# The norm behind attention and the last output tile worked in two halves of the tokens, with residual updates written through a PSUM bank

## What is computed

```python
x = x + g1 * rms_norm(y_lat, mix_post_g[i])        # y_lat = o @ w_o, behind attention
f_lat = conv_ffn(modulate(rms_norm(x, ffn_pre_g[i]), sh2, sc2), *ffn)
x = x + g2 * rms_norm(f_lat, ffn_post_g[i])        # the output

def conv_ffn(h, w_up, w_dw, b_dw, w_down):
    gate, val = jnp.split(h @ w_up, 2, axis=-1)
    gate = depthwise_conv(gate, w_dw) + b_dw        # width 3, along the tokens
    return (jax.nn.gelu(gate) * val) @ w_down
```

## Time and profile before

| What | Value |
|---|---|
| three runs | 1698.0, 1706.21, 1707.32 us; median 1706.21 us |
| profiled execution | 1699.19 us, of which the span of its instructions is 1697.4 us |
| PE busy in the span | 1606.5 us (95%) |
| DVE, ACT and POOL busy | 737.4, 734.3 and 822.1 us (43, 43 and 48%) |
| chain that ended last | PE 79%, DVE 7%, issue 5%, DMA 3%, POOL 3%, ACT 2% |

### The profile page before, as it was taken

The page is one execution under the profiler, slowest core; times in us unless marked ns, Lnnn a source line. Parts: engine busy times, 40 slices in busy tenths (PEclk is TensorE's granted clock), DMA queues, the critical chain, the costliest instruction groups (busy, mean ns, idle before and its releaser), DMA issues.

```text
span 1697.4 us, 25340 instructions
## 1 busy us (share of the span) xinstructions
PE 1606.5 (95%) x9293; PEld 1283.3 (76%) x9293; DVE 737.4 (43%) x1384; ACT 734.3 (43%) x1093; POOL 822.1 (48%) x444
## 2 busy tenths in 40 slices
PE   6789999999999999999999999999996999999996
PEld 2676656769998888888888687777774888888885
DVE  3574796664457444344442714454333433333002
ACT  3431343555765555454322425454453544443221
POOL 1453334558788744444445543242524344444553
PEclk8899999999999999999999999999997999999998
DMA  9677777455565523232774231111112233233321
GB/s 385 205 211 215 208 216 215 137 186 179 180 188 151 152 93 99 87 99 83 284 267 160 83 102 45 48 39 56 45 36 77 65 97 98 88 98 93 100 80 49
DMA packets 71651, 224.82 MB, mean 132 GB/s; under 512 B 8080, under 2 KB 15760, under 8 KB 71312
## 3 DMA queue, kind: packets, MB, share of 16 engines
q1 hardware_dynamic: 68832, 215.72, 40.9%
q10 hardware_dynamic: 2736, 7.95, 1.3%
HBM read 218.13 MB, written 5.51 MB: 132 GB/s over the span
## 4 chain that ended last, share of the span: by engine, by line
PE 79%; DVE 7%; issue 5%; DMA 3%; POOL 3%; ACT 2%; SPq 1%; DVEq 0%; ACTq 0%; POOLq 0%
PE bank L1657 20%; PE bank L1655 20%; PE bank L1656 20%; PE bank L1625 2%; POOL bias L753 2%; PE bank L1975 2%; DVE bank L1316 1%; PE bank L1977 1%; DVE x_lat L1223 1%; PE bank L1976 1%; PE bank L2048 1%; PE bank L2058 1%; PE bank L1599 1%; DMA squares_lat<-in_mod_w 1%; PE bank L1818 1%
## 5 line engine op out<-in xcount | busy, mean ns | idle before, releaser
L657 POOL TENSOR_TENSOR w_lo<-w_raw,w_hi 128x1024 fp32r<-128x1024 f32 (+1 forms) x288 | 686.4, 2389 | 718.1 <-ACT w_hi L815 718.0
L815 ACT ACTIVATE w_hi<-w_raw 128x1024 fp32r<-128x1024 f32 (+1 forms) x288 | 298.8, 1038 | 239.7 <-PE bank L1657 189.7
L1657 PE MATMUL bank<-h_hi_lat,w_lo 128*128 128x512 f32 x856 | 336.9, 394 | 0.0
L1655 PE MATMUL bank<-h_hi_lat,w_hi 128*128 128x512 f32 x856 | 335.8, 392 | 0.6 <-DVE u_lat L1340 0.6
L1656 PE MATMUL bank<-h_lo_lat,w_hi 128*128 128x512 f32 x856 | 335.3, 392 | 0.0
L1655 PEld LDWEIGHTS bank<-h_hi_lat,w_hi 128*128 128x128 f32 x856 | 160.7, 188 | 49.3 <-issue 11.3
L1656 PEld LDWEIGHTS bank<-h_lo_lat,w_hi 128*128 128x128 f32 x856 | 160.7, 188 | 36.4
L1657 PEld LDWEIGHTS bank<-h_hi_lat,w_lo 128*128 128x128 f32 x856 | 160.9, 188 | 33.0
L1655 PE MATMUL bank<-h_hi_ctx,w_hi 128*128 128x256 f32 x544 | 157.2, 289 | 11.1 <-DVE h_lo_ctx L1247 7.3
L1657 PE MATMUL bank<-h_hi_ctx,w_lo 128*128 128x256 f32 x544 | 153.6, 282 | 0.0
L1656 PE MATMUL bank<-h_lo_ctx,w_hi 128*128 128x256 f32 x544 | 153.6, 282 | 0.0
(11 more groups left out here) (224 smaller groups left out, 2708.1 us busy)
## 6 DMA issues: line engine op xcount, KB each, us to landing
w_raw<-in_ffn_w_up SPq DMA_DIRECT2D x132, 512.0 KB, 3.5
w_raw<-in_cv_w_pw SPq DMA_DIRECT2D x48, 512.0 KB, 5.6
w_raw<-in_ffn_w_down SPq DMA_DIRECT2D x48, 448.0 KB, 3.4
ada_raw<-in_mod_w SPq DMA_DIRECT2D x40, 512.0 KB, 6.9
mod_rows<-in_mod_rows SPq DMA_DIRECT2D x32, 512.0 KB, 5.8
w_raw<-in_ffn_w_down SPq DMA_DIRECT2D x24, 512.0 KB, 3.6
shifted_lat<-u_lat SPq DMA_DIRECT2D x32, 270.0 KB, 6.6
w_raw<-in_na_w_qk SPq DMA_DIRECT2D x16, 512.0 KB, 4.0
```

Of the source, the lines that this page charges most:

```text
L657: pool.tensor_tensor(wlo[s][:, 0:kt * P], raw[s][:, 0:kt * P], whi[s][:, 0:kt * P].bitcast(F32), ALU.subtract).then_inc(w_lo, 1)
L815: act.activation(whi[s][:, 0:kt * P], raw[s][:, 0:kt * P], ACT.Copy).then_inc(w_hi, 1)
L1655: pe.matmul(b, whi[s][:, w], hi[:, a], start=(first and k == 0), stop=False)
L1657: ins = pe.matmul(b, wlo[s][:, w], hi[:, a], start=False, stop=(last and k == kts - 1))
```

## The change

The chain behind attention is worked in two halves of 256 tokens, and the halves are laid past one another.

- **PE.** The second round of `o` makes the first half of all four blocks, then the second half. The first half's sum of y squares and its spread are put inside the second half's matmuls. The first round of `up1` starts three blocks on the first half, with the other half's spread among them, then the fourth; the second half starts with two blocks, the first gate and value pair, which is signalled before the other pair is begun.
- **DVE, ACT, POOL.** Each step of the chain handles 256 tokens, in an order written out by hand. In the first half the scaled y is written to a PSUM bank and added to x from there. In the second half the even tiles go that way on DVE, and POOL adds the odd ones. ACT loads the table for gelu at the end of the chain, ahead of the first gate.
- **The last tile.** The eighth tile of `down1` is made half by half in two banks, and the sum and spread of the first half are put inside the second half's matmuls. DVE and POOL update x half by half. The stores become sixteen of 128 KB; the odd tiles are issued by ACT instead of SP.

The diff, cut:

```diff
+        LAST, RINV_OF = [bank[3], bank[5]], [bank[6], bank[7]]
...
+        def half_of(k, h):
+            return slice(k * L + h * HALF, k * L + (h + 1) * HALF)
+        def half_rows(h):
+            return slice(h * 2 * BLK32, (h + 1) * 2 * BLK32)
...
+            for h in range(2):
+                for k in range(0, KD, 2):
+                    sp.wait_ge(x_up, fin.up0 + h * (KD // 2) + k // 2 + 1)
+                    sp.dma_start(out_t[:, half_of(k, h)], X[LAT][:, half_of(k, h)]).then_inc(stored, 16)
+            sp.wait_ge(stored, 32 * KD)
...
+            def o_halves(ph, base):
+                def add_half(h, j):
+                    part = half_of(0, h)
+                    pool.wait_ge(summed, base + 5 + 4 * h + j)
+                    pool.tensor_tensor(acc[LAT][:, part], acc[LAT][:, part], sq[j % 2][:, part],
+                                       ALU.add).then_inc(summed, 1)
+                for j in range(4):
+                    pool.wait_ge(o_half_ev, j + 1)
+                    add_half(0, j)
+                for j in range(4):
+                    pool.wait_ge(evac, ph.evac0 + 4 + j + 1)
+                    add_half(1, j)
+                    lo_ahead(ph, 1, j, True)
+                for k in range(1, KD, 2):
+                    tile = half_of(k, 1)
+                    pool.wait_ge(al_y, KD + k + 1)
+                    pool.tensor_tensor(X[LAT][:, tile], X[LAT][:, tile], al.Y[:, tile], ALU.add).then_inc(al_x_odd, 1)
...
+                        if name == "down1" and (it, j) == (1, ph.per - 1):
+                            for h in range(2):
+                                part = half_of(0, h)
+                                pool.wait_ge(evac, ph.evac0 + KD + h)
+                                pool.tensor_tensor(acc[side][:, part], acc[side][:, part], sq[1][:, part],
+                                                   ALU.add).then_inc(summed, 1)
...
+            def o_halves(ph, q0, hi_ahead):
+                def half_out(h, j):
+                    act.wait_ge(summed, q0 + 4 + 4 * h + j)
+                    part = half_of(0, h)
+                    act.activation(al.Y[:, half_of(4 + j, h)], bank[j][:, part], ACT.Copy)
+                    return act.activation(sq[j % 2][:, part], bank[j][:, part], ACT.Square)
+                def out_b(j):
+                    act.wait_ge(blk, ph.blk0 + 4 + j + 1)
+                    half_out(1, j).then_inc(evac, 1)
+                for j in range(4):
+                    act.wait_ge(o_half, j + 1)
+                    half_out(0, j).then_inc(o_half_ev, 1)
+                al_root(0, 1)
+                out_b(0)
+                hi_ahead(ph, 1, 0, True)
+                al_squares(0, 0, 2)
+                out_b(1)
+                hi_ahead(ph, 1, 1, True)
+                al_squares(0, 2, 5)
+                out_b(2)
+                hi_ahead(ph, 1, 2, True)
+                al_squares(0, 5, 8)
+                al_root(0, 2)
+                out_b(3)
+                hi_ahead(ph, 1, 3, True)
+                al_hi_h(0, 0, 2)
+                al_root(1, 1)
+                al_hi_h(0, 2, 8)
+                al_squares(1, 0, 8)
+                al_root(1, 2)
+                al_hi_h(1, 0, 8)
+                act.activation(act_spacer[:, :], ident[:, 0:1], ACT.Gelu_apprx_tanh)
...
+                        if name == "down1" and (it, j) == (1, ph.per - 1):
+                            act.wait_ge(summed, q0 + KD - 1)
+                            for h in range(2):
+                                part = half_of(0, h)
+                                act.wait_ge(last_half, h + 1)
+                                act.activation(Y[:, half_of(KD - 1, h)], LAST[h][:, part], ACT.Copy)
+                                act.activation(sq[1][:, part], LAST[h][:, part], ACT.Square).then_inc(evac, 1)
+                                if h == 0:
+                                    root_half(fin, 0)
...
             y_phase("o", "kq")
-            post_now(al)
-            pre_now(al)
             up_phase("up1", "o", 1)
             y_phase("down1", "up1")
-            root(chains["out_l"], 1, RMS_EPS)
+            root_half(fin, 1)
+            for h in range(2):
+                for k in range(1, KD, 2):
+                    act.wait_ge(x_up_odd, h * (KD // 2) + k // 2 + 1)
+                    act.dma_start(out_t[:, half_of(k, h)], X[LAT][:, half_of(k, h)]).then_inc(stored, 16)
...
+            def scaled_y(k, h):
+                return al.Y[:, half_of(k, h)] if h and k % 2 else bank[5][:, half_of(0, k % 2)]
+            def al_update(h):
+                dve.wait_ge(al_spread, 2 * h + 1)
+                for t in range(KD // 2):
+                    for k in (2 * t, 2 * t + 1):
+                        y = al.Y[:, half_of(k, h)]
+                        if not h and k >= 2:
+                            dve.wait_ge(al_x, k - 1)
+                        elif h and k % 2 == 0:
+                            dve.wait_ge(al_x, KD + k // 2)
+                        dve.scalar_tensor_tensor(scaled_y(k, h), y, drv[:, al.gain + k:al.gain + k + 1],
+                                                 RINV_OF[h][:, half_of(0, h)], ALU.mult, ALU.mult).then_inc(al_y, 1)
+                    for k in (2 * t,) if h else (2 * t, 2 * t + 1):
+                        xk = X[LAT][:, half_of(k, h)]
+                        dve.wait_ge(al_y, h * KD + k + 1)
+                        dve.tensor_tensor(xk, xk, scaled_y(k, h), ALU.add).then_inc(al_x, 1)
+            def al_scale(h):
+                dve.wait_ge(al_spread, 2 * h + 2)
+                for k in range(KD):
+                    tile = half_of(k, h)
+                    dve.scalar_tensor_tensor(SQ[LAT][:, tile], X[LAT][:, tile], drv[:, al.pre[0] + k:al.pre[0] + k + 1],
+                                             RINV_OF[h][:, half_of(0, h)], ALU.mult, ALU.mult).then_inc(al_t, 1)
+            def al_low(h):
+                for k in range(KD):
+                    tile = half_of(k, h)
+                    dve.wait_ge(al_hi, h * KD + k + 1)
+                    dve.scalar_tensor_tensor(Hlo[LAT][:, tile], SQ[LAT][:, tile],
+                                             mod[:, al.pre[1] + k:al.pre[1] + k + 1],
+                                             Hhi[LAT][:, tile].bitcast(F32), ALU.add, ALU.subtract).then_inc(al_lo, 1)
+            al_recip(0, 1)
+            al_update(0)
+            al_recip(0, 2)
+            al_scale(0)
+            al_recip(1, 1)
+            al_low(0)
+            al_update(1)
+            al_recip(1, 2)
+            al_scale(1)
+            al_low(1)
...
             up_phase("up1", 1, sum0["down1"])
             fin = chains["out_l"]
+            for h in range(2):
+                rows_ = half_rows(h)
+                dve.wait_ge(rms, fin.rms0 + h + 1)
+                dve.reciprocal(inv_t[rows_, :], root_t[rows_, :]).then_inc(rcp, 1)
+                dve.wait_ge(spread, fin.spread0 + h + 1)
+                for t in range(KD // 2):
+                    for j in range(2):
+                        y = fin.Y[:, half_of(2 * t + j, h)]
+                        dve.scalar_tensor_tensor(y, y, drv[:, fin.gain + 2 * t + j:fin.gain + 2 * t + j + 1],
+                                                 RINV_OF[h][:, half_of(0, h)], ALU.mult, ALU.mult).then_inc(y_sc, 1)
+                    xk = X[LAT][:, half_of(2 * t, h)]
+                    dve.wait_ge(y_sc, fin.up0 + h * KD + 2 * t + 1)
+                    dve.tensor_tensor(xk, xk, fin.Y[:, half_of(2 * t, h)], ALU.add).then_inc(x_up, 1)
...
+            def o_by_halves(ph):
+                for j in range(4):
+                    split_wait(ph, 1, j)
+                    pe.wait_ge(evac, ph.evac0 + j + 1)
+                    half_products(bank[j], ph.slot(j), Ohi, Olo, 0, 0, KD).then_inc(o_half, 1)
+                between_parts = {0: (4, lambda: al_sum(0)), 1: (2, lambda: al_inverse(0, 1))}
+                for j in range(4):
+                    pe.wait_ge(o_half_ev, j + 1)
+                    k = 0
+                    if j in between_parts:
+                        k, step = between_parts[j]
+                        half_products(bank[j], ph.slot(j), Ohi, Olo, 1, 0, k)
+                        step()
+                    half_products(bank[j], ph.slot(j), Ohi, Olo, 1, k, KD).then_inc(blk, 1)
+                al_sum_squares(0)
+                al_sum(1)
+                al_inverse(0, 2)
+            def up_by_halves(ph):
+                hi, lo = Hhi[LAT], Hlo[LAT]
+                for h in range(2):
+                    if h:
+                        al_sum_squares(1)
+                        al_inverse(1, 2)
+                    else:
+                        split_wait(ph, 0, 2)
+                        pe.wait_ge(evac, ph.evac0)
+                    together = range(2 if h else 3)
+                    for k in range(KD):
+                        pe.wait_ge(al_hi, h * KD + k + 1)
+                        for j in together:
```

(47 more changed lines are left out.)

162 lines of the change are left out of this document (107 added, 55 removed).

## The result

| | Time | Profiled execution | Its span |
|---|---|---|---|
| before | 1702.82 us (median of 10 runs, 1698.0 to 1707.32) | 1699.19 us | 1697.4 us |
| changed | 1689.81 us (median of 10 runs, 1684.13 to 1695.14) | 1689.66 us | 1687.6 us |

The ratio is 0.9923, with a 95% interval of 0.9906 to 0.9941: 13.0 us faster, between 10 and 16. The two profiled spans differ by 9.8 us. That difference can't be taken as the change's own, since the changed kernel's profiled execution comes 2.25 us later to the place where the change begins: `o`'s second round starts at 1270.95 there and at 1268.70 before.

The account below looks back on a forecast made before the run. PE carries nearly the whole span, so only its waits behind `o` (24.7 us) and at the end (16.9 us) count. 12.8 - 1.7 (clock) + 3.9 (tail) - 0.9 (handoffs) = 14.1 us; from mean 1702.7, 1688.6 us, range 1681 to 1698.

Parts of the forecast that it names:

- the tail: Last tile to the end of the span: halving it gains 3.9 us, between 2.5 and 4.9.
- the fall of the clock: In PE's gaps behind `o` and inside `up1`'s first round: one fall to half speed taken, costing 1.7 us.
- second part: `up1` by halves: second round starts at 1326.9 against 1339.73, 12.8 us gained; later by 5 us or more refutes it.
- The sum of squares: In the norm, ahead of each of PE's two gaps: 32 pieces for one half take some 1.2 us.
- The bounds of the clock: Both PE gaps: loss from nothing to 3.4 us if both trigger a fall; clock low less than 4 us a gap.
- Rival (d): Each gap has a clock fall and the tail gains its lower bound: gain 10, 1692.5 us; chance 0.11.
- The added wait: Gap behind `o`: PE takes the second half's y sum before the first half's spread, which ends at 1297.1, not 1296.4.
- The first pair and the table: `up1`'s first round: gelu loads leave the first pair's path; product takes 6.5 us, PE waits 0.9; loads would cost 2.6.
- The bank: First half's update: DVE additions with an operand in a bank take 0.40 to 0.43 us, not blocked by POOL.
- rival (a): First half's update: bank does not spare DVE, eight additions cost 11.6 us more; gain 4, 1699 us; chance 0.06.
- Rival (b): ACT late, halves do not interlock: each gap 8 us instead of 5.1 and 4.3; gain 7.5, 1695 us; chance 0.10.
- Rival (c): Clock low from the first gap until `up1`'s first round is done: loss of 6.8 us, 1709.5 us; chance 0.05.

Follow-up runs that it names:

- e10: Changed kernel with each half's partition sums and spread over four groups of 64 tokens, not two of 128; 63.17 us from `o`'s to `up1`'s second round.
- e2: Changed kernel with the last tile and stores of before, so only the chain behind attention is halved; 1693.57 us, ratio 0.9955 to the kernel before.
- e6: Changed kernel with ACT's copy of the fourth block's second half ahead of the first half's second root; ratio 0.9918 to the kernel before.
- e7: Changed kernel with the fourth block's first half (24 matmuls) left for the gap inside `up1`'s first round; 58.79 us from `o`'s to `up1`'s second round.
- e9: e7's edit plus, in the changed kernel's gap behind `o`, earlier squares and root, sum between matmuls, later second-half y sum; 1684.38 us, ratio 0.9885 to before.
- e11: e9 with the norm's sums laid on four groups of 64 tokens instead of two of 128; 1685.55 us, ratio 0.9896 to the kernel before.
- e4: Changed kernel without ACT's early gelu, so the tables load inside the first gate's work; 64.46 us from `o`'s to `up1`'s second round.

## Why the prediction came out

The prediction said 1688.6 us and a gain of 14.1; 1689.8 and 13.0 were measured, and the two profiles give about 12 for the pieces: the stretch gained 8.84 where the sum had 10.2 (12.8 - 1.7 - 0.9), the tail 3.3 where it had 3.9. That the times agree to 1.2 us is in part luck, since the interval of 10 to 16 us can't tell 14 from 12. The steps are a sharper test. Counted from the start of `o`'s second round, where the prediction has 1268.70 and the changed trace 1270.95:

| Step | Predicted | Measured |
|---|---|---|
| first spread starts | 16.0 | 16.4 |
| first update ends | 23.1 | 23.0 |
| second half's y sum starts | 27.6 | 28.6 |
| PE restarts behind `o` | 29.5 | 30.9 |
| sum of gap 2 starts | 41.6 | 43.0 |
| PE resumes behind gap 2 | 45.8 | 48.2 |
| first gate | 51.7 | 55.6 |
| second round of `up1` | 58.2 | 62.2 |

The predicted column is the layout alone, without the fall of the clock (1.7) and the handoffs (0.9), which the prediction takes off in its sum. By the trace's own clock the second round starts at 1333.14, 6.2 us behind the predicted 1326.9, and the prediction had called 5 us a refutation of its second part. But 2.25 of these lie ahead of the change, so counted from the same start it is 4.0, a near miss of that sign.

- **The sum of squares was the mis-sized term.** I priced it at 1.2 us from the sixteen pieces of 0.65, which are two tiles' and not one's. Those ran over four groups of columns; a half uses two groups, and its 32 pieces take 1.94. Twice 0.74 is 1.5 us of the 4.0 by which the second round is late, and about the 1.4 by which the stretch gained less than the sum had. e10 shows the cause: the same data over four groups take 1.10.
- **The fall of the clock** was priced at 1.7 and cost 1.5 to 1.6 us in the changed kernel's profile, in gap 2. That this profile shows one fall, neither none nor two, nothing in the rows foretold; it is luck. The added handoffs were put at 0.9, and what is left of the 4.0 is about 1.0. Both terms came out in size, but that remainder was not taken apart by any run.
- **The bounds of the clock were too narrow.** Twelve profiles have these two gaps: six show no fall, four a fall in one gap and two in both. Where it fell in gap 1, it was low for 6.8 us and cost 2.5 to 2.9, against the 1.7 per gap and the "less than 4 us a gap" of the prediction. Both together cost some 4 us, not 3.4. The Trainium skill, "TensorE: Matmul & The Clock Gate", section "HAM oscillation — how this bites in real kernels", would have each gap pay each time if its wait is long enough; the trace agrees in two runs of twelve. The same code can fall or not: gap 2 is the same in e2, which shows none, and in the changed kernel. But the edits may matter too. All five profiles of e6, e7, e9 and e11, which take a wait out of a gap or fill one, show no fall, and six of the other seven show one or two; four of the five without a fall are from one chip. What decides between edit, chip and chance is not shown. Rival (d) came by half in the changed kernel's profile: one fall, and a tail above its lower bound.
- **The added wait** behind POOL's sum was put at 0.7 us. In the trace the reciprocal ends at 1299.17 and the spread starts at 1299.93: 0.76. e6 got 0.7 to 0.96 back by taking it away. That step held.
- **The first pair and the table** held: product 6.53 us from the gate (6.5 predicted), PE's wait 0.94 (0.9), the table 2.47 in e4 (2.6).
- **The bank** held, and rival (a) with it fell: the additions took 0.41 to 0.42 us each, a pair 0.74. But its price was too high. Without the bank only the additions that met POOL's steps were slow, 4.5 us on DVE instead of 11.6.
- **Rival (b)**, halves that don't interlock, did not come: gaps of 5.9 and 5.1 us instead of 5.1 and 4.3, both longer by the sum of squares. **Rival (c)**, the low clock through all of the first round, did not come in any run.
- **The tail** gained 3.3 us against 3.9, in range. The first half went as laid out (DVE done 18.9 us behind the last tile's start, 18.8 predicted). The second spread took 1.22 us instead of 0.65, because the clock fell while PE waited (the first half's, also four pieces, took 0.71); ahead of it, ACT's copy behind PE's second half came 17.0 us behind the tile's start instead of 16.4. The store is about 0.3 shorter, which I had left out.

## What to carry to other kernels

Cutting a serial chain in two pays as far as each half's steps stand under the other half's matmuls; price each step at the halved shape, since a step whose speed comes from working side by side (groups of columns, partitions) does not get cheaper by half the data. Laid over all groups and partitions with half the columns, the sum took 1.10 us instead of 1.94 and the reciprocal 0.55 instead of 0.95. Where a gap stays, look for matmuls that are done ahead of it and could stand in it: moving 24 of them into gap 2 was worth 1.4 us with nothing else changed. And take the time from pieces of several profiles when run-to-run variation lies outside the piece.

## What was not expected of the hardware

- **A partition sum of half the tokens takes as long as one of all.** A y sum of four pieces in two column groups takes 0.41 us, and before, one of eight pieces in four groups took 0.43:

```profile
1683.00 0.43 PE L1786 MATMUL bank<-feature_sum_lat,ones 128*32 128x128 f32 x8 [2.52 <-POOL feature_sum_lat L683]
```

The squares' 32 pieces take 1.94 in two groups and 64 pieces 1.10 in four. The reciprocal of 64 partitions took 0.95 us, as that of 128 did; with 64 columns instead of 128 it took 0.55.
- **The variation between executions lies upstream of the change.** In eleven of the twelve profiles of the changed kernel and its variants with both gaps, the time between second round and tail is 325.8 us to within 0.02 (in the twelfth, e4, the clock fell once more there). The point where the stretch begins, however, wanders from 1266.0 (e6's first profile) to 1274.9 us (e11). From 60 us to 1280 the clock is low for 13.6 us in the first and for 27.3 in the second; at half speed the 13.7 us between them would be 6.8 of those 8.9 us (an estimate from these two figures). One place where they part, e6's first profile, then e11:

```profile
276.00:280.00 4.00, 2.42 (x22) 1.00 1.05 297
280.00:284.00 4.00, 4.00 (x44) 1.00 0.78 307
```

```profile
280.00:284.00 4.00, 1.10 (x13) 0.87 1.04 244
284.00:288.00 4.00, 4.00 (x20) 0.50 1.01 404
```

PE waits ahead of the same instruction in both, 1.57 us in the first (until 278.74) and 2.90 in the second (until 283.94), and the clock falls in the second alone. At the same place e2 waits 2.78 us with a fall, and the kernel before 2.83 without one, so the length of the wait alone doesn't decide it. Why PE waits longer there in one execution than in the next was not tried.
